# The first products of two stages put into the gap of the finish ahead of them, and the first tile's rest on VectorE

## The reference, cut to what matters

```python
for layer in range(DEPTH):
    h = rmsnorm(x, pre_norm_w[layer])
    ...
        y = hgrn2_mixer(h, lower_bounds[layer], rec_w_in[j], rec_gnorm_w[j], rec_w_out[j])
    x = x + rmsnorm(y, post_norm_w[layer])
...
h = _rmsnorm(x, norm_w)
u = (h @ w_in).astype(f32)
gla_u, rwkv_u = u[..., :GLA_IN], u[..., GLA_IN:]
```

## Time and profile before

| | us |
|---|---|
| median of three runs | 3682.74 (3682.12 to 3684.82) |
| the profiled execution | 3683.04 |
| its span | 3681.7 |
| TensorE busy | 3506.7 (95%) |
| VectorE, ScalarE, GpSimd busy | 2060.8, 1719.7, 1356.1 |

### The profile page before, as it was taken

How to read it: one execution, slowest core, us unless ns; L and a number is a source line. 1 busy time by engine, 2 the same in 40 slices (tenths; PEclk the granted TensorE clock), 3 DMA queues, 4 the chain that set the end, 5 groups by cost and what they waited for, 6 DMA issues and landing times. The chain is left out here.

```text
span 3681.7 us, 83160 instructions
## 1 busy us (share of the span) xinstructions
PE 3506.7 (95%) x34784; PEld 2822.9 (77%) x34784; DVE 2060.8 (56%) x4661; ACT 1719.7 (47%) x3161; POOL 1356.1 (37%) x1684
## 2 busy tenths in 40 slices
PE   8999998898999999999998989999999997999999
PEld 7878786687887877878786877777777776788777
DVE  4566766645655556555555445766666665343422
ACT  3455555522555556555553344444444442444422
POOL 5433321132545454545543323232222220444332
PEclk9999999999999999999998999999999998999999
DMA  4322211223010111101112341111111113322322
GB/s 136 90 66 81 61 53 32 83 91 106 26 44 24 41 30 30 41 24 41 30 34 83 131 146 48 39 43 40 43 43 43 42 37 111 86 70 70 104 80 92
DMA packets 251987, 231.26 MB, mean 63 GB/s; under 512 B 9120, under 2 KB 222560, under 8 KB 251616
## 3 DMA queue, kind: packets, MB, share of 16 engines
q1 hardware_dynamic: 251616, 225.94, 20.2%
HBM read 192.35 MB, written 33.55 MB: 61 GB/s over the span
## 5 line engine op out<-in xcount | busy, mean ns | idle before, releaser
L195 PE MATMUL bank<-hT_cut,arena_cut 128*128 128x512 f32 x2080 | 818.2, 393 | 0.0
L188 ACT ACTIVATE arena<-bank 128x512 f32<-128x512 f32 (+1 forms) x584 | 315.8, 570 | 588.4 <-PE bank L196 303.1
L194 PE MATMUL bank<-hT_cut,arena_cut 128*128 128x512 f32 x1240 | 554.3, 447 | 0.5 <-issue 0.5
L194 PE MATMUL bank<-arena_cut,hT_cut 128*128 128x512 f32 (+1 forms) x1280 | 461.0, 360 | 33.0 <-DVE arena_cut L1140 28.4
L196 PE MATMUL bank<-hT_cut,arena_cut 128*128 128x512 f32 x1240 | 488.6, 394 | 0.0
L188 ACT ACTIVATE arena<-arena 128x512 f32<-128x512 f32 (+3 forms) x674 | 350.0, 555 | 246.3 <-POOL arena L1509 191.7
L195 PEld LDWEIGHTS bank<-hT_cut,arena_cut 128*128 128x128 f32 x2080 | 394.4, 190 | 80.4 <-issue 19.3
L195 PE MATMUL bank<-arena_cut,hT_cut 128*128 128x512 f32 (+1 forms) x1280 | 449.2, 351 | 0.0
L189 ACT ACTIVATE arena<-arena 128x256 f32<-128x256 f32 (+2 forms) x336 | 210.2, 626 | 420.2 <-DVE arena L178 193.2
L194 PE MATMUL bank<-oT_cut,arena_cut 128*128 128x512 f32 x840 | 363.7, 433 | 7.3 <-POOL arena_cut L2760 4.3
L2760 POOL TENSOR_TENSOR arena_cut<-arena,arena_cut 128x256 fp32r<-128x256 f32 x272 | 218.5, 833 | 409.7 <-ACT arena_cut L188 409.7
(11 more groups left out here) (259 smaller groups left out, 7149.2 us busy)
## 6 DMA issues: line engine op xcount, KB each, us to landing
arena<-in_w_in SPq DMA_DIRECT2D x100, 512.0 KB, 3.9
arena<-in_attn_w_in SPq DMA_DIRECT2D x144, 256.0 KB, 2.8
arena<-in_rec_w_in SPq DMA_DIRECT2D x64, 512.0 KB, 4.0
x_after<-arena SPq DMA_DIRECT2D x32, 512.0 KB, 2.6
arena<-x_after SPq DMA_DIRECT2D x32, 512.0 KB, 4.1
arena<-in_x SPq DMA_DIRECT2D x16, 512.0 KB, 3.6
h_after<-hT SPq DMA_DIRECT2D x4, 2048.0 KB, 7.7
hT<-h_after SPq DMA_DIRECT2D x4, 2048.0 KB, 16.8
```

Of the source, the lines that this page charges most:

```text
L188: return e.activation(out, a, f, bias=bias, scale=scale)
L194: pe.matmul(out, a[0], b[0], start=start, stop=False)
L195: pe.matmul(out, a[0], b[1], start=False, stop=False)
```

## The change

Two classes, `RecurrenceHead` and `DeltaHead`, put steps of the following stage among those of the finish ahead of it. `in_turn` calls them as `ahead(t)` behind `rest(t - 1)`. SyncE loads the first weights at t = 5, ScalarE rounds them (t = 7 and 8, or 8 and 10) and 512 columns of hT (t = 12 and 13), GpSimd subtracts the weights' rest (t = 8 to 12), VectorE hT's rest (t = 12 to 14: two, three and three instructions), and TensorE multiplies at t = 15, between the transposes of tile 14 and those of tile 15: f and q of unit 0 (48 products) ahead of the recurrence, block w and half of block k (36 products) ahead of the delta rule. Weights and rounded parts lie in tiles of oT that have been used. `recurrence` and `delta_rule` leave these steps out, TensorE no longer settles there, and the selection table is loaded in four pieces per partition. In all three finishes VectorE makes the rest of o's tile 0, which GpSimd made.

```diff
+    cut_by = lambda t: c_p.by("lo", t - 1) if t else c_v.by("lo")
...
-    def in_turn(cut, first, rest):
+    def in_turn(cut, first, rest, ahead=None):
...
             if t:
                 rest(t - 1)
+            if head is not None and ahead is not None:
+                ahead(t)
         rest(NT - 1)
...
-            pe.wait_ge(*c_p.by("lo", t))
+            pe.wait_ge(*cut_by(t))
...
-        cut(0)
         cut(1)
         k.settle(pool)
...
+        v.wait_ge(*c_a.by("hi", 0))
+        v.tensor_tensor(part(k.oT_cut, 0), part(k.oT, 0), part(k.hT_cut, 0), ALU.subtract).then_inc(*c_v.did("lo"))
         for n, c in enumerate(early + later):
...
+class RecurrenceHead:
...
+    def on_sp(self, t):
+        if t == 5:
+            self.k.sp.wait_ge(*self.products_of(3))
+            for i, _ in self.order:
+                src = self.k.columns_of(self.k.ins["rec_w_in"][0], i * D, RK)
+                self.k.sp.dma_start(self.raw[i], src).then_inc(*self.got[i].did("in"))
...
+    def on_dve(self, t):
+        v = self.k.dve
+        for c in {12: (0, 1), 13: (2, 3, 4), 14: (5, 6, 7)}.get(t, ()):
+            v.wait_ge(*self.h_a.by("hi", c))
+            v.tensor_tensor(self.h_lo[:, c, :], self.h[:, c, :], self.h_hi[:, c, :], ALU.subtract).then_inc(*self.h_v.did("lo"))
...
+    def on_pe(self, t, last_use):
+        pe = self.k.pe
+        if t < NT - 1:
+            return
+        for n, (i, name) in enumerate(self.order):
+            pe.wait_ge(*last_use(n))
+            pe.wait_ge(*self.rest[i].by("lo"))
+            for c in range(KC):
+                if n == 0:
+                    pe.wait_ge(*self.h_v.by("lo", c))
+                ins = product(pe, self.k.bank[n], (self.hi[i][:, c, :], self.lo[i][:, c, :]),
+                              (self.h_hi[:, c, :], self.h_lo[:, c, :]), start=(c == 0), stop=(c == KC - 1))
+            ins.then_inc(*self.products.did(name))
...
-        k.settle(pe)
-
         def project(i, name, u):
...
         def front(u):
             for i, name in pieces:
-                yield from project(i, name, u)
+                if u or i not in early:
+                    yield from project(i, name, u)
+            if u == 0:
+                pe.wait_ge(*banks_free[1])
...
-        sp.dma_start(k.oT[:, 0:2, 0:width // 2], k.ins["select"].rearrange("p (a n) -> p a n", a=2)).then_inc(*sel_got.did("in"))
+        sp.dma_start(sel_at, k.ins["select"].rearrange("p (a n) -> p a n", a=4)).then_inc(*sel_got.did("in"))
...
+class DeltaHead:
...
+    def on_sp(self, t):
+        if t != 5:
+            return
+        sp, w_in = self.k.sp, self.k.ins["w_in_2"][0]
+        sp.wait_ge(*self.products_of(3))
+        src = w_in[:, self.columns[0]:self.columns[0] + P].rearrange("(a b p) n -> p a b n", p=P, b=2)
+        for b in range(2):
+            sp.dma_start(self.raw[0][:, :, b * P:(b + 1) * P], src[:, :, b]).then_inc(*self.got[0].did("in"))
+        sp.wait_ge(*self.products_of(7))
+        sp.dma_start(self.raw[1].rearrange("p (c n) -> p c n", c=KC), self.k.columns_of(w_in, self.columns[1], P)).then_inc(*self.got[1].did("in"))
```

More of the change, by code:

```diff
@@ L264, in loads, with phase @@
         return self.steps(name, "in", each=16)
-    def phase(self):
-        self.before = [s.end() for s in self.every if s.n]
-        self.every, self.used, self.table = [], 0, None
+    def phase(self, kept=()):
+        self.before = [s.end() for s in self.every if s.n and s not in kept]
+        self.every, self.used, self.table = list(kept), 0, None
     def settle(self, *engines):
@@ L1003, in on_sp @@
             sp.dma_start(at, src.unsqueeze(0).broadcast_to([P, D])).then_inc(*r_got.did("in"))
-        in_turn(nothing, first, rest)
+        in_turn(nothing, first, rest, ahead=lambda t: nxt.on_sp(t))
     def on_pe():
@@ L1038, in on_pe @@
         k.settle(pe)
-        in_turn(nothing, first, rest)
+        in_turn(nothing, first, rest, ahead=lambda t: nxt.on_pe(t, last_use))
     def on_act():
@@ L1144, in on_dve @@
         v.wait_ge(*r_got.end())
-        in_turn(nothing, nothing, rest)
+        in_turn(nothing, nothing, rest, ahead=lambda t: nxt.on_dve(t))
+    if head is not None:
+        nxt = head(k, lambda t: m_pe.by("m1", t), lambda t: N["hT"].by("h1", t))
+        k.head = nxt
     on_sp()
@@ L1151, in finish_layer @@
     on_dve()
+    k.banks_free = [y_ok.end(), N["hT"].end()] if next_w is not None else []
     k.freed = [m_pe.end()]
@@ L1157, in recurrence @@
 def recurrence(k):
-    freed, ready = k.freed, k.ready
-    k.phase()
+    freed, head, banks_free = k.freed, k.head, k.banks_free
+    early = [i for i, _ in head.order]
+    k.phase(head.kept)
     nc, pe, a, v, pool, sp = k.nc, k.pe, k.act, k.dve, k.pool, k.sp
@@ L1241, in on_sp @@
         for i, _ in pieces:
-            load(i, 0)
+            if i not in early:
+                load(i, 0)
         k.before.append(k.last_store())
@@ L1479, in back @@
             yield
[L1481 to L1487, removed]
+        for i, _ in pieces:
+            if i not in early:
+                split(i, 0)
         k.settle(a)
@@ L1650, in back @@
             v.wait_ge(*Bv.by("on", u))
+            if u == 0:
+                v.wait_ge(*Fpe.by("q", 1))
             stt(v, k.oT[:, h, cols(g)], e_of(u, 6), gn, z, ALU.mult, ALU.mult).then_inc(*Bv.did("out"))
             yield
[L1654 to L1657, removed]
         k.settle(v)
@@ L2415, in block @@
             b = bank(fb, kind, g if p is None else 4 * g + p)
+            if n == 0:
+                return
             pe.wait_ge(*w_p.by("lo", n))
-            for c in range(KC):
+            for c in range(head.half if n == 1 else 0, KC):
+                if n == 1:
+                    ins = head.piece(1, c)
+                    if c == KC - 1:
+                        ins.then_inc(*steps.did(kind))
+                    yield
+                    continue
                 if kind == "w":
@@ L2462, in front @@
                 yield from block("k", g, p, Fpe)
+                if u == 0:
+                    for done in banks_free:
+                        pe.wait_ge(*done)
                 gates()
@@ L2745, in carry @@
             yield
[L2747 to L2750, removed]
         k.settle(a)
         a.wait_ge(*set_v.by("kept3"))
-        in_turn(nothing, solve, scores, carry, front)
+        in_turn(solve, scores, carry, front)
     def on_pool():
         def split(n):
-            if n < len(blocks):
+            if len(head.raw) <= n < len(blocks):
                 pool.wait_ge(*w_a.by("hi", n))
@@ L2972, in carry @@
             yield
-        for done in ready:
-            v.wait_ge(*done)
-        run(cut(0))
         k.settle(v)
```

182 lines of the change are left out of this document (143 added, 39 removed).

## The result

| | us |
|---|---|
| median, changed kernel | 3691.53 (3686.33 to 3696.88, 15 runs) |
| median, kernel before | 3681.22 (3676.52 to 3684.82, 15 runs) |
| ratio | 1.0032, 95% interval 1.0025 to 1.0039 |
| profiled execution, changed | 3695.83, span 3694.4 |

The change makes the kernel slower, by 0.3%: the medians are 10.3 us apart, the ratio says 11.8 (9.2 to 14.4). Forecast was 3690.9, 8.2 more than the median of three runs that stood for before; 3691.53 is nearer to it than the sum deserves, since before came out 1.5 lower in 15 runs.

What follows compares the result with a forecast made beforehand. The prediction took TensorE, busy nearly throughout, as the bound, with time won only where it idles or runs at its lower clock. Terms -2.0 - 1.8 + 11.5 + 0.5 = +8.2 gave 3690.9 us; range 3685.5 to 3695.0.

Steps and rivals of the forecast that it cites:

- Term 3: Second finish: SyncE's wait for tile 7's products delays tile 6's x, so TensorE idles 9.0 us and restarts slowly; +11.5 us.
- Term 2: f and q ahead of the recurrence: f of unit 1 starts 4.3 us earlier but slowly, 2.5; net -1.8 us.
- Term 4: w and half of k ahead of the delta rule: first mix waits for the table, r starts earlier but slowly; +0.5 us.
- Term 1: Starts of the three finishes: tile 0's rest on VectorE lets TensorE start earlier, -0.7 us each, -2.0 in all.
- (a): Rival, second finish: SyncE's wait is covered because x 6 is already in place; 3679.4 us, chance 0.07.
- (b): Rival, both stage starts: the setups keep up with TensorE, tables' landings not holding ab and first mix; 3665.2 us, chance 0.04.
- (c): Rival, second finish: the stall comes twice, x 7 or x 8 also late, or landings slow; 3695 us, chance 0.10.

Runs made afterwards that it cites:

- stall_alone: The kernel before plus only SyncE's wait for tile 7's products ahead of the load of tile 6's x in the second finish; 3690.12 us.
- both_setups: bounds_first plus, at the delta rule, h's last store behind the load of z's weights and VectorE's table wait at its first scan; 3667.97 us.
- all_early: both_setups plus h's next 512 columns rounded ahead of the bounds and z's weights rounded ahead of the norm's root; 3655.35 us.
- bounds_first: late_load with VectorE making the gate's bounds ahead of its waits for the tables in the recurrence's setup; 3675.22 us.
- h_early: both_setups with the rounding of h's next 512 columns moved ahead of the bounds on ScalarE, rests right behind on VectorE; 3661.87 us.
- late_load: The changed kernel with SyncE's wait and the load of block k's weights moved from step 5 to step 9 of the second finish; 3679.25 us.

## Why the prediction was right, step by step

| term | forecast | measured | how |
|---|---|---|---|
| 1, tile 0 on VectorE | -2.0 | -2.9 | the waits for w_out's rest, 25.5 for 28.4 |
| 2, f and q ahead | -1.8 | -1.1 | +0.80, -5.19 and +3.34, below |
| 3, SyncE's wait | +11.5 | +11.95 | B, 120.55 for 108.60 |
| 4, w and half of k ahead | +0.5 | +0.83 | C, 44.28 for 43.45 |
| sum | +8.2 | +8.8 | medians: +10.3 |

**Term 3** was the forecast, and was right in place, cause and size: SyncE issued the load at 2073.12, which is where tile 7's products end; VectorE's addition had waited 14.05 us. The idle time is 10.30 (9.0 forecast): I had two issues and the median landing of 4.1, and left out that block k's load travels ahead of x, which took 5.6. The slow start is 11.95 - 10.30 = 1.65 (2.5 forecast). The two errors nearly cancel, and that is luck. Both controls, the wait alone and the change without it, agree.

**Term 2** has three parts. VectorE's rests of h delay the transposes of tiles 13 and 14, each by 0.34 (12.41 for 12.07 behind those of the tile before): from the first product to tile 14's transposes it is 194.60 for 193.80, +0.80 (0.9 forecast, over three tiles). From there to f of unit 1 it is 33.40 for 38.59; the `ab` forecast at 924.6 came at 924.04, and f of unit 1 starts 933.38 - 705.38 = 228.00 after the first product, for 232.39: 4.39 earlier (4.3 forecast), at the end of the chain that I had costed row by row. The restart costs more: from f of unit 1 to where TensorE begins to wait for the second finish it is 1973.38 - 5.31 - 933.38 = 1034.69 for 1975.91 - 6.35 - 938.21 = 1031.35, so 3.34 (2.5 forecast, from one example). What was off is that size, by 0.8.

The Trainium skill, "TensorE: Matmul & The Clock Gate", What's actually happening, calls this share variable from run to run. Here it varies between places, 1.65 and 3.34 us in one kernel; the granted clock is 0.50 for 3 us behind one gap and for 6 behind the other. Between executions I see no variation in the few that were profiled: A, with the slow restart in it, is 1268.00, 1268.00 and 1267.98 in the three kernels that share it, one execution each.

**Term 4** had the tables' landing as what holds the first mix (8.3 forecast, 9.0 measured) and a slow r (its first ten products start 0.43 apart, from 2208.12 on). What I had not said is that the gates wait as well for `in_rwkv_a_up`, behind the same store; it decided nothing here, since the mix was as late. The gap before z grew from 1.98 to 3.39 us, but that is not the new slow start that I had feared: the clock fell behind the shorter one too. The size is near the spread of C: with the change's code C is 44.28, 44.56 and 43.88 in three kernels, with the code of before (in two of them with the setup edits) 43.40 to 43.57 in five, so it is 0.8 more in the mean; stall_alone, at 44.98, stands outside both.

**Term 1** was sized as 0.7 a finish and is 0.8 to 1.0 (9.08, 6.35, 8.15 to 8.32, 5.31, 7.13). In the second and third finish the mechanism was right: VectorE's first rest of w_out fell from 2.89 and 3.03 us to 1.22. In the first finish it was not. There GpSimd's rests of tiles 0 and 1 had run beside VectorE's last steps of the attention and not beside w_out's rests, the first of which took 1.21. Before, in VectorE's timeline:

```profile
700.61 3.07 DVE L805 TENSOR_TENSOR oT<-oT,hT 128x768 f32<-128x768 f32 x1
...
703.93 9.37 DVE L1140 TENSOR_TENSOR arena_cut<-arena,arena_cut 128x1024 fp32r<-128x1024 f32 x8
```

and now:

```profile
699.51 0.96 DVE L805 TENSOR_TENSOR oT<-oT,hT 128x768 f32<-128x768 f32 x1
...
701.85 15.72 DVE L1148 TENSOR_TENSOR arena_cut<-arena,arena_cut 128x1024 fp32r<-128x1024 f32 x8
```

The attention's last steps got shorter, the first rest of w_out now takes 3.38 beside GpSimd's rest of tile 1, and the difference happens to be of the forecast size. The Trainium skill, "SBUF — State Buffer", Who interferes with whom, would have such instructions block each other wherever they meet, and the trace agrees: the slowest of the 24 rests still takes 3.42. The sharing is not gone; it is moved, in two finishes of three behind the start.

**What is not in the sum.** The profiled execution has a span 12.7 us over that of before, and the terms make 8.8. From z to the first product of gla it is 920.86 us for 916.27, 4.6 more, nearly all of it in the last 70 us of the delta rule (71.87 for 67.38). In the eleven experiments this stretch is 915.8 to 918.6. Some of it may belong to the gap before z (918.2 to 918.6 in three kernels that have it, 917.05 in the fourth; but 918.40 in one that has it not). No run settles this; the medians, 10.3 apart, leave 1.5 for it.

**The rivals.** (a) SyncE's wait covered: out. (b) The setups keep up: not in this kernel, but its mechanism is real. Moving waits and one store (both_setups) brings about half of it, and two more edits of the order in ScalarE's and VectorE's lists bring the rest: all_early measured 3655.35, and the rival's sum without term 3 is 3682.7 - 27.0 - 2.0 = 3653.7. I said that both tables would have to be there much sooner. That was the wrong condition, and my description of the kernel was wrong where it has the bounds made out of the tables: neither the bounds nor the first mix reads a table. They were only listed behind the waits for it. (c) A second stall: out; tile 7's transposes follow without a gap.

## What to carry to other kernels

Work moved into an idle stretch is worth what the next thing to come allows: price the chain that it used to cover, and mend that chain in the same change (here 1.3 and nothing apart, 6.5 together). A wait in the list of the engine that issues all DMAs delays every load behind it; put it where it is fulfilled already. Ask of each wait at a stage's start whether the instruction behind it reads what is waited for, and let large stores that nobody awaits go last.

## What the runs showed of the hardware that was not expected

A remaining gap of 3.4 us costs TensorE the same slow restart as one of 8.8: from f of unit 1 to the second finish's wait it is 1034.69 us in the changed kernel and 1964.37 - 5.31 - 924.20 = 1034.86 in bounds_first. Behind 1.98 us (before z, in the kernel before) the clock was at 0.50 too; behind a wait of 0.49 (h_early) it stays at 1.00. A gap is worth closing whole.

The start of the second finish has two lengths with the same code: from its first product to tile 5's transposes it is 87.48 us in the kernel before and 85.39 in stall_alone, 87.49 in the changed kernel and 85.29 in late_load. The waits for w_out's rests differ with it, 8.3 and 6.7 us in the first pair, 7.7 and 5.9 in the second. What differs is how many of VectorE's last rests of w_out run beside GpSimd's for tiles 2 and 3: in the changed kernel the last two take 3.4 us each, in late_load only the last. GpSimd begins there 7.51 and 7.70 us after the first product. In the eleven kernels with tile 0's rest on VectorE the longer start goes with 7.48 to 7.51 and the shorter with 7.63 or more; in the kernel before and stall_alone it is 6.97 and 7.89. That moment hangs on ScalarE, whose roundings of tiles 2 and 3 stand behind those of w_out's last two blocks, and these wait for their loads (0.41 and 0.21 us in the changed kernel, 0.56 and 0.22 in late_load). So a load that lands 0.2 us sooner goes with a start that is 2 us longer. No run moved that load on purpose.
